# A projection result made in two steps of four input tiles instead of three of 3, 3 and 2, in the group B passes of a streaming encoder

## The reference

```python
qa, ka, va, qb, kb, vb = [t.reshape(B, T, -1, HEAD_DIM) for t in split_cols(h @ w_in, EVEN_SPLITS)]
...
def stick_breaking(q, k, v, q_pos, k_pos):
    z = jnp.einsum('bqhd,bkhd->bhqk', q, k, preferred_element_type=jnp.float32) * (q.shape[-1] ** -0.5)
    vis = k_pos[None, :] < q_pos[:, None]
    log_beta = jnp.where(vis, jax.nn.log_sigmoid(z), NEG_INF)
    log_keep = jnp.where(vis, jax.nn.log_sigmoid(-z), 0.0)
    later = lax.cumsum(log_keep, axis=3, reverse=True) - log_keep
    w = jnp.exp(log_beta + later)
    return jnp.einsum('bhqk,bkhd->bqhd', w.astype(v.dtype), v)
```

## Time and profile before

| | |
|---|---|
| median of 3 timed runs | 3404.33 us (3401.92 to 3407.5) |
| profiled execution, its own time | 3405.78 us |
| its span | 3404.2 us |
| mean granted TensorE clock | 0.969 |
| the three passes with the change | 464.4 to 726.4 us |

### The profile page before, as it was taken

One profiled execution on the slowest core, in us unless ns is written; L12 is line 12 of the kernel. 1 busy time (PEld: TensorE's weight loads), 2 busy tenths in 40 slices (PEclk: granted clock), 3 DMA queues, 4 the chain that ended last, 5 costly groups with the idle time before them and its releaser, 6 DMA issues. The chain is left out here.

```text
span 3404.2 us, 49900 instructions
## 1 busy us (share of the span) xinstructions
PE 3075.7 (90%) x17776; PEld 2606.5 (77%) x17776; DVE 1468.2 (43%) x2858; ACT 1086.4 (32%) x2601; POOL 576.8 (17%) x352
## 2 busy tenths in 40 slices
PE   5777788888889999999999979988979999999996
PEld 4666667765589999999976645555559999999996
DVE  4232347775344344333351434445434344333335
ACT  3333357764232221222220023345423222222221
POOL 2111111100132222222210000000013222222220
PEclk8999999999999999999999999989989999999998
DMA  2111111100111111111111010000011111111111
GB/s 88 35 37 37 39 43 35 35 23 23 44 38 44 45 44 45 45 44 45 38 37 37 19 35 8 6 4 19 28 41 38 44 45 50 39 45 44 45 38 53
DMA packets 52801, 127.68 MB, mean 38 GB/s; under 512 B 11760, under 2 KB 19968, under 8 KB 52640
## 3 DMA queue, kind: packets, MB, share of 16 engines
q1 hardware_dynamic: 44160, 108.33, 9.9%
q0 software_dynamic: 5312, 16.80, 1.4%
q10 hardware_dynamic: 3168, 0.18, 0.1%
HBM read 111.52 MB, written 13.76 MB: 37 GB/s over the span
## 5 line engine op out<-in xcount | busy, mean ns | idle before, releaser
L1366 PE MATMUL ps<-hh,wh 128*128 128x384 f32 (+1 forms) x2112 | 698.7, 331 | 38.6 <-POOL hl L113 31.7
L1366 PE MATMUL ps<-hl,wh 128*128 128x384 f32 (+1 forms) x2112 | 698.1, 331 | 0.0
L1366 PE MATMUL ps<-hh,wl 128*128 128x384 f32 (+1 forms) x2112 | 697.3, 330 | 0.0
L1493 POOL TENSOR_TENSOR wl<-raw,wh 128x1024 fp32r<-128x1024 f32 x132 | 330.0, 2500 | 1123.6 <-ACT wh L1419 1123.6
L1366 PEld LDWEIGHTS ps<-hh,wh 128*128 128x128 f32 x2112 | 401.7, 190 | 42.7 <-issue 42.7
L1536 DVE TENSOR_SCALAR gates<-u,par 128x1090 f32<-128x1090 f32 x88 | 74.6, 848 | 775.0 <-ACT tail L1444 775.0
L1366 PEld LDWEIGHTS ps<-hh,wl 128*128 128x128 f32 x2112 | 401.8, 190 | 0.0
L1366 PEld LDWEIGHTS ps<-hl,wh 128*128 128x128 f32 x2112 | 400.4, 190 | 0.0
L225 PE MATMUL pot<-hh_mix,wh_mix 128*128 128x384 f32 (+1 forms) x576 | 209.1, 363 | 65.9 <-ACT q_next L261 22.6
L1419 ACT ACTIVATE wh<-raw 128x1024 fp32r<-128x1024 f32 x132 | 138.8, 1052 | 337.0 <-PE pot L1385 193.3
L225 PE MATMUL pot<-hl_mix,wh_mix 128*128 128x384 f32 (+1 forms) x576 | 192.4, 334 | 0.0
(11 more groups left out here) (267 smaller groups left out, 5753.9 us busy)
## 6 DMA issues: line engine op xcount, KB each, us to landing
raw<-in_ffn_w SPq DMA_DIRECT2D x132, 512.0 KB, 3.3
w<-in_w SPq DMA_DIRECT2D x64, 256.0 KB, 2.6
w<-in_w SPq DMA_DIRECT2D x12, 512.0 KB, 3.6
w<-in_w_out SPq DMA_DIRECT2D x16, 256.0 KB, 2.7
strip<-in_bias POOLq DMA_DIRECT2D x5, 640.0 KB, 4.2
x<-in_x SPq DMA_DIRECT2D x4, 768.0 KB, 9.3
out_y<-x SPq DMA_DIRECT2D x2, 1536.0 KB, 6.6
out_bv<-vt POOLq DMA_DIRECT2D x4, 512.0 KB, 3.0
```

The source lines that it names most:

```text
L1366: mm = e.matmul(bank[:, 0:b - a], w[:, n % 3, k * P:(k + 1) * P], x[:, k, a:b], start=k == 0 and first, stop=k == KT - 1 and w is m.wl)
L1493: e.tensor_tensor(m.wl[:, n % 3, :], m.raw[:, n % 3, :], m.wh[:, n % 3, :].bitcast(F32), ALU.subtract).then_inc(self.low, 1)
```

## The change

In the passes of group B with a next pair, the 8 input tiles of a result are shared out over its three steps as 4, 4 and 0 instead of 3, 3 and 2.

```diff
             if more and -1 <= s < 26:
                 n, part = divmod(s + 1, 3)
-                st.products(e, j + self.p0 + 1, KT * n + (0, 3, 6)[part], KT * n + (3, 6, 8)[part])
+                st.products(e, j + self.p0 + 1, KT * n + (0, 4, 8)[part], KT * n + (4, 8, 8)[part])
             elif not more and 0 <= s < self.per:
```

## The result

The changed kernel takes 3430.77 us (median of 4 runs, 3430.29 to 3434.22), against 3403.18 us for the kernel before, measured beside it (4 runs, 3401.92 to 3407.5): the ratio is 1.0076, with a 95% interval of 1.0063 to 1.0089. It is slower, by some 26 us by the ratio and 27.6 by the medians, more than twice the 11.8 us of the prediction's sum and outside its range. The profiled execution has a span of 3429.4 us, 25.2 more than before.

What follows compares the result with a forecast made beforehand. The prediction took the order in which PE, ACT and DVE hand on work as the bound. Delays of 3.94 us a pass over three passes, 11.8 us, gave 3416 us for the median; range 3405 to 3427 us, chance 0.74.

Steps and rivals of the forecast that it cites:

- The circle of PE, ACT and DVE: Group B passes: PE transposes, ACT reads, works on with DVE, copies the result; projection matmuls ahead of the transpose add delay.
- Result 2: Boundary before result 2: first-step transpose of result 1 comes later, +0.53 us; postponed scores may add a few tenths, not summed.
- The terms: Delays before results 2 to 7 from later transposes: 0.53, 0.34, 0.53, 1.05, 0.44 and 1.05 us, together 3.94 us a pass.
- Result 3: Boundary before result 3: second-step transpose of result 2 comes 0.88 us later, 0.54 us of it hidden, +0.34 us.
- Result 8: Boundary before result 8: DVE's copy ends while PE is still at transposes that come no later, 0 us.
- the sum's silence on the clock: The sum over three passes, 11.8 us, counted only later transposes and no fall of the clock in mid-pass.
- a rival with a chance of 0.05: Longer PE waits bring one more 6.8 us half-clock stretch into every pass: 10 us more, 3426 us; chance 0.05.
- The signs in the profile: PE waits before results 5, 7, 4: about 1.2, 2, 1.3 us; new 0.5 before result 3; L1006 little changed or more; passes 91.
- the case that the prediction gave for being wrong: Passes staying at 87 us, ACT's copies starting earlier within a pass, or the clock falling in mid-pass.
- Swallowed idle time: ACT and DVE catch up between boundaries and PE's idle time hides the delay: 3404 to 3411 us; chance 0.19.
- Copy in the rest: Finished result is copied while it rests in the third step, removing waits before L225: 3392 us; chance nearly all of 0.07.
- Nothing covered: Each of 8 boundaries in a pass pays its whole third step, 24 us in all: 3428 us; chance 0.08.

Runs made afterwards that it cites:

- experiment 4: Input tiles split 3, 4, 1 instead of 3, 3, 2 in the kernel before: only second-step transposes later; 3409.15 us, ratio 1.0009.
- experiment 5: Input tiles split 4, 2, 2 instead of 3, 3, 2 in the kernel before: only first-step transposes later; 3414.69 us, ratio 1.0021.
- experiment 2: Changed kernel plus one useless 256-column matmul behind the transposes of each third step; 3422.32 us, ratio 1.0045 to the kernel before.
- experiment 6: Input tiles split 3, 5, 0 instead of 3, 3, 2 in the kernel before: second-step transposes six matmuls later; 3421.37 us, ratio 1.0048.
- the filled kernels: Changed kernel with two (experiment 1) or one (experiment 2) useless matmuls in each third step; both ratio 1.0045 to the kernel before.
- experiment 1: Changed kernel plus two useless 256-column matmuls behind the transposes of each third step; 3419.43 us, ratio 1.0045 to the kernel before.
- experiment 8: Changed kernel with each result's copy moved to the head of its own third step; 3408.02 us, ratio 1.0005 to the kernel before.

## Why the prediction was wrong

**The circle of PE, ACT and DVE: right.** The chains were read from which transpose ACT had waited for. All six boundaries with a price grew, and all but result 2 within 0.13 us of the forecast wherever the clock held. Experiments 4 and 5 take the two steps apart: results 5 and 7 hang on the second step, 4 and 6 on the first. Result 2 hangs on both.

**The terms: 3.94 us a pass forecast, 4.6 measured** (experiment 2). Result 2 was 0.81 instead of 0.53. Two chains end there. The one from the first step's transpose was read rightly: experiment 5 moves it alone and has 0.51. The other starts from the scores behind the second step's matmuls: it costs 0.27 with three matmuls more ahead of them (experiment 4) and 0.82 with six (experiment 6), so some 0.25 us of a delay is hidden. In the changed kernel the later of the two counts, not their sum, and that is the scores: the same Relu waits 0.19 us for L994 there. The prediction named them as "a few tenths" and left them out of the sum. Result 3 was 0.47 for 0.34. Result 8 was 0.30 for 0: experiment 5, without filler and with only the first step packed, has the same 0.30, so the term that was put at nothing hangs on the first step; by which path isn't shown.

**The step that failed: the sum's silence on the clock.** "If waits now of up to 2.3 us brought one more such stretch of 6.8 us into every pass" was a rival with a chance of 0.05, priced at 10 us. It is what happened, in seven stretches of 3.4 us. Even this rival's price, 3426 us, is under the measured time, since it stood on the sum's 11.8 us of order. The ledger of the profiled execution: 3 x 4.6 = 13.8 us of order, 7 x 1.5 = 10.5 us of clock, and -0.7 us ahead of result 1's start and behind result 8's, where the passes open and close, together 23.6 of the 23.8 measured. Taken one by one, the seven intervals with a stretch exceed those of experiment 2 by 1.46 to 1.56 us. By the ratios of the timed runs the filled kernels are 15 us above the one before and the changed one 26 us. With the granted clocks of experiment 1 this puts some 11 us on the clock there too. The mistake was in the evidence: that the clock stayed up through waits of 1.31 us was taken to say that it would through longer and more frequent ones, though the sum itself said that the waits would grow to 2 us. The Trainium skill, TensorE: Matmul & The Clock Gate, section A second HAM failure mode, tells of frequent micro-idles between matmul groups that make the clock swing. The trace of the changed kernel agrees with it, with its seven stretches in mid-pass, where that of the kernel before had none to show.

**The signs in the profile.** Result 5's wait rose to 1.20, result 7's to 2.02, result 4's stayed at 1.31, and one of 0.8 us stands before result 3, as announced. ACT's total wait for L1006 grew by 13.3 us. The passes are 94 to 96 us long, not 91, and the clock fell in mid-pass: the case that the prediction gave for being wrong. With the clock held up, in experiment 2, result 1 of one pass and of the next lie some 91.5 us apart, which is what the chains had said.

**The rivals.** Swallowed idle time: wrong, every boundary shows its growth. Copy in the rest: wrong, and experiment 8 shows that even with the copy moved the time ends where that of the kernel before is. Nothing covered: its 24 us is near the measured time, but not its mechanism, since results 4 and 6 pay three matmuls, not six.

**What stays open.** Which waits bring the clock down. In the profiled executions, of the waits of 1.31 us ahead of result 4, two of three were followed by a stretch in the changed kernel, one of three in experiment 5, and none in the kernel before and in experiments 4 and 6. Of the three of 2.07 us two were, of the six of 2.02 us (changed kernel and experiment 6) all; waits of 1.57 to 1.69 us (experiments 2 and 4 to 6) brought none. So the length of the wait alone doesn't decide. Shown is that every mid-pass stretch begins at the end of such a wait or within 1.4 us behind it, and that filling the waits, or taking them away from the results as in experiment 8, ends the stretches. Where the clock fell in the timed runs of 4, 2, 2 isn't seen either.

## What to carry to other kernels

On an engine that shares its time between free work and a chain through other engines, work is covered only where it stands behind the instruction that the others wait for. Moving it ahead costs its full duration, less what slack the chain has, at each boundary whose chain starts there, whatever the busy shares say: PE was busy 88% and ACT and DVE some 71% of the pass here. Where two chains end at one boundary, the later one sets the price. Before moving work together, look for the consumer: finishing a result sooner is worth nothing while its reader's place in its own order is fixed, and a gap that opens on TensorE may have to be priced twice, as a wait and as the matmuls that run at half clock behind it. That the clock held through the gaps of the present kernel is no evidence for longer ones.

## What the runs showed of the hardware

Seven of nine waits of 1.31 to 2.07 us, between dense runs of matmuls, were followed in the changed kernel by a stretch of 3.4 us at the 1.2 GHz clock, each worth an estimated 1.5 us, though TensorE was busy 85% of the pass. Waits of 1.31 us in the kernel before and of 1.31 to 1.57 us in experiment 4 were not. Two useless matmuls in each third step kept the clock at 1.00 within the passes and made the kernel about 11 us faster than without them. At half clock a matmul of 384 columns started 0.32 us after the one before, at full clock 0.175 us.
